# Linear attention inside a three-block kernel: blocks of 32 tokens centred on their middle, a predicated copy for the mask, three span levels above

## What is computed

```
A[t, s] = sum over d of  q[t, d] * k[s, d] * exp(c[t, d] - c[s, d])     for s <= t, else 0
out[t]  = sum over s of  A[t, s] * v[s]
```

## Time and profile before

| | us |
|---|---|
| runs, median (lowest to highest) | 2513.09 (2512.47 to 2515.55) |
| the profiled execution, its own time | 2516.41 |
| its span | 2514.6 |
| PE busy | 2092.3 (83%) |
| DVE busy | 513.2 (20%) |
| ACT busy | 367.6 (15%) |
| POOL busy | 318.8 (13%) |

### The profile page before, as it was taken

The page is one execution under the profiler, slowest core; times in us unless marked ns, Lnnn a source line. Parts: engine busy times, 40 slices in busy tenths (PEclk is TensorE's granted clock), DMA queues, the critical chain, the costliest instruction groups (busy, mean ns, idle before and its releaser), DMA issues.

```text
span 2514.6 us, 34562 instructions
## 1 busy us (share of the span) xinstructions
PE 2092.3 (83%) x14302; PEld 1163.0 (46%) x14303; DVE 513.2 (20%) x1073; ACT 367.6 (15%) x815; POOL 318.8 (13%) x144
## 2 busy tenths in 40 slices
PE   6987778677878857988879798899979899888888
PEld 5765322122222212322238675789965546454444
DVE  1044411001111101111120464100031201241111
ACT  1231111001101100111111423100001112210001
POOL 4100122222221222212210000000000000001221
PEclk9978689889999988999989969999979999989999
DMA  9654699999998899998934635455524334249994
GB/s 320 163 202 154 254 429 416 429 426 410 415 421 355 375 429 426 377 395 346 388 125 134 228 108 201 171 163 143 159 84 147 104 126 158 103 198 364 413 413 163
DMA packets 183210, 681.36 MB, mean 271 GB/s; under 512 B 15906, under 2 KB 57139, under 8 KB 150112
## 3 DMA queue, kind: packets, MB, share of 16 engines
q1 hardware_dynamic: 179200, 670.02, 68.1%
q0 software_dynamic: 3920, 10.24, 1.7%
q10 hardware_dynamic: 16, 0.02, 0.0%
HBM read 679.18 MB, written 1.06 MB: 271 GB/s over the span
## 4 chain that ended last, share of the span: by engine, by line
PE 62%; DMA 24%; DVE 7%; ACT 3%; SPq 2%; issue 1%; POOL 1%; DVEq 0%; POOLq 0%; ACTq 0%
PE ps L749 31%; DMA scr<-in_w_mlp 11%; PE ps L1092 8%; DMA MOD<-in_w_mlp 7%; PE ps L1118 5%; DMA HTY<-in_w 2%; PE ps L1396 2%; DMA spare<-in_b_mlp 2%; PE ps L784 2%; PE ps L1129 2%; PE ps L1060 1%; PE ps L1096 1%; PE ps L890 1%; PE ps L828 1%; PE ps L1433 1%
## 5 line engine op out<-in xcount | busy, mean ns | idle before, releaser
L1092 PE MATMUL ps<-ring,scr 128*32 128x512 f32 x2208 | 304.3, 701 | 139.7 <-POOL ring L696 139.0
L749 PE MATMUL ps<-ring,HTY 128*128 128x512 f32 (+5 forms) x960 | 328.0, 503 | 6.8 <-DMA ring<-in_w_out 3.7
L696 POOL COPY ring<-scr 128x4096 f32<-128x4096 f32 x62 | 223.0, 3600 | 759.1 <-DMA scr<-in_w_mlp 616.0
L749 PEld LDWEIGHTS ps<-ring,HTY 128*128 128x128 f32 x960 | 175.3, 191 | 155.9 <-issue 141.0
L1092 PEld LDWEIGHTS ps<-ring,scr 128*32 128x32 f32 x2208 | 74.5, 123 | 364.1 <-POOL ring L696 189.5
L749 PE MATMUL ps<-HTY,ring 128*128 128x256 f32 (+1 forms) x1072 | 238.1, 385 | 1.8 <-ACT HTY L1477 1.8
L749 PEld LDWEIGHTS ps<-HTY,ring 128*128 128x128 f32 (+1 forms) x1072 | 205.4, 192 | 33.3 <-ACT HTY L1477 2.7
L2199 DVE TENSOR_SCALAR spare<-ps 128x256 f32<-128x256 f32 x46 | 19.5, 425 | 686.3 <-PE ps L1096 686.3
L1477 ACT ACTIVATE scr<-ps 128x512 f32<-128x512 f32 (+6 forms) x118 | 58.4, 497 | 504.8 <-PE ps L749 401.3
L749 PE MATMUL ps<-ring,scr 128*128 128x128 f32 (+1 forms) x1040 | 121.6, 280 | 1.4 <-DVE scr L2304 1.4
L749 PEld LDWEIGHTS ps<-ring,scr 128*128 128x128 f32 x1040 | 117.5, 192 | 5.2 <-issue 3.3
(11 more groups left out here) (426 smaller groups left out, 2000.2 us busy)
## 6 DMA issues: line engine op xcount, KB each, us to landing
scr<-in_w_mlp SPq DMA_DIRECT2D x94, 2048.0 KB, 25.3
ring<-in_w_mlp SPq DMA_DIRECT2D x34, 2048.0 KB, 20.7
MOD<-in_w_mlp SPq DMA_DIRECT2D x32, 2048.0 KB, 24.2
HTY<-in_w_mlp SPq DMA_DIRECT2D x32, 2048.0 KB, 22.1
ring<-in_w_ada SPq DMA_DIRECT2D x23, 2048.0 KB, 9.1
ring<-in_w_in SPq DMA_DIRECT2D x20, 2048.0 KB, 7.9
ring<-in_w_ff SPq DMA_DIRECT2D x16, 2048.0 KB, 9.0
ring<-in_w SPq DMA_DIRECT2D x16, 2048.0 KB, 15.9
```

What stands on the lines that cost most here:

```text
L696: pool.tensor_copy(m1_slabs[j], m1_arrivals[j]).then_inc(moved[j], 1)
L749: mm = pe.matmul(o, lhs(k), rhs(k), start=begin and k == 0, stop=end and k == nk - 1)
L1092: mm = pe.matmul(ps[C1 * c:C1 * (c + 1), 0, :], XG[:, 2 * j + i, :], m1_slabs[j][:, i, BANK * c:BANK * (c + 1)], start=j + i == 0, stop=False)
```

## The change

For block one the four lower levels (16, 8, 4 and the parts) are replaced by one product over the whole tile, with decays taken relative to the middle token of each block of 32: exp(c[t] - c[mid]) goes to the query (`QB`), exp(c[mid] - c[s]) to the key (`KB`). The product is right inside each block of 32; the spans of 64 and 32 overwrite their rectangles in the same PSUM bank. A predicated copy with an integer mask of s <= t moves what is valid into `AT`, which POOL has set to zero. Level 128 stays as it was. Block two keeps all levels and the parts.

The order moves too: DVE weighs in `between(1)`, and the gain on the gate goes to `between(2)`; ACT's exponentials stand ahead of the modulations in `between(1)`; PE's and ACT's linear products stand ahead of the modulations in `between(2)`. `STAGES` follows: four products instead of seven.

```diff
-    ("ada1b", [2] * 6, 7), ("ada1c", [2] * 2, 2), ...
+    ("ada1b", [2] * 4, 4), ("ada1c", [2] * 4, 2), ...
+CENTERED = 32
+LEVELS_OF = (WIDE[:3], LEVELS)
...
 # POOL, behind vector(3)
+            pool.wait_ge(product_free, end["in1"])
+            pool.memset(AT[1], 0.0).then_inc(zeros_ready, 1)
...
 # PE
+            def centered_products():
+                pe.wait_ge(lin["spans_weighed"], 1)
+                for h in range(2):
+                    hs = slice(64 * h, 64 * h + 64)
+                    b = bank()
+                    for tile in range(NT):
+                        for pair in range(2):
+                            c, t = P * (2 * tile + pair), slice(P * tile, P * (tile + 1))
+                            mm = pe.matmul(b[:, c:c + P], KB[hs, pair, t], QB[hs, pair, t], start=True, stop=True)
+                            for i in range(1, len(LEVELS_OF[0])):
+                                m = LEVELS_OF[0][i]
+                                for row in range(0, P, 2 * m):
+                                    n = m * (P * tile + row) // (2 * m)
+                                    mm = pe.matmul(b[row:row + m, c + row + m:c + row + 2 * m], KL[hs, i, pair, n:n + m],
+                                                   QL[hs, i, pair, n:n + m], start=True, stop=True)
+                    close(mm)
+                for h in range(2):
+                    hs = slice(64 * h, 64 * h + 64)
+                    b = bank()
+                    for pair in range(2):
+                        mm = pe.matmul(b[:, P * pair:P * (pair + 1)], KL[hs, 0, pair, :], QL[hs, 0, pair, :], start=True, stop=True)
+                    close(mm)
             def rest_of_modulation(i):
+                if i == 2:
+                    centered_products()
                 for x in range(2):
                     modulation("ada1b", 0, 4 + 2 * i + x)
-                if i == 2:
-                    linear_products(0)
...
 # ACT
+            def centered_decays():
+                act.wait_ge(lin["spans"], 1)
+                act.activation(KL[:, 0:3], KL[:, 0:3], ACT.Exp)
+                act.activation(QL[:, 0:3], QL[:, 0:3], ACT.Exp)
+                act.activation(KB, QB, ACT.Exp, scale=-1.0)
+                act.activation(QB, QB, ACT.Exp).then_inc(lin["span_exp"], 1)
+            def centered_products():
+                for h in range(2):
+                    read(NB[:, h], product().rearrange("p (t c n) -> p t c n", t=NT, c=2))
+                for h in range(2):
+                    read(AT[0][:, h:4:2, P:S], two(product(), P))
             def rest_of_modulation(i):
+                if i == 1:
+                    centered_decays()
+                if i == 2:
+                    centered_products()
                 modulation(0, 4 + 2 * i)
                 modulation(0, 5 + 2 * i)
-                if i == 1:
-                    decays(0)
-                if i == 2:
-                    linear_products(0)
...
 # DVE; spans and weigh_spans now run over LEVELS_OF[n]
+            def weigh_centered():
+                weigh_spans(0, GQ, GK)
+                step(dve.tensor_tensor(KB, KB, GK, ALU.mult))
+                tell(dve.tensor_tensor(QB, QB, GQ, ALU.mult), lin["spans_weighed"], 1)
...
+            def merge_centered():
+                dve.wait_ge(product_free, end["ada1b"])
+                dve.wait_ge(zeros_ready, 6)
+                shape = [P, 2, 2, P]
+                for tile in range(NT):
+                    a = AT[tile][:, :, 0:P].rearrange("p (c h) n -> p h c n", h=2)
+                    tell(dve.copy_predicated(a, INCL.unsqueeze(1).unsqueeze(1).to_broadcast(shape), NB[:, :, tile]), lin["merged"], tile + 1)
             def between_windows(i):
                 if i == 0:
+                    middle = centered(CUM)[:, :, :, CENTERED // 2 - 1:CENTERED // 2].to_broadcast([P, 2, S // CENTERED, CENTERED])
+                    step(dve.tensor_tensor(centered(QB), centered(CUM), middle, ALU.subtract))
                     spans(0, CUM)
-                    parts(0, CUM)
+                    step(dve.tensor_tensor(INCL, tri[:, :], ident[:, :], ALU.add))
                 if i == 1:
+                    weigh_centered()
+                if i == 2:
                     gh = GG.rearrange("p a (h d) -> p a h d", h=4)
                     step(dve.tensor_tensor(gh, gh, gla_norm.unsqueeze(1).unsqueeze(1).to_broadcast([P, NT, 4, P]), ALU.mult))
-                if i == 2:
-                    weigh_parts(0, GQ, GK)
-                    weigh_spans(0, GQ, GK)
                 if i == 3:
-                    merge(0, end["ada1b"])
+                    merge_centered()
```

More of the change, by code:

```diff
@@ L55 @@
 LEVELS = WIDE + NARROW
+CENTERED = 32
+LEVELS_OF = (WIDE[:3], LEVELS)
 STAGES = [
     ("ada1a", [2] * 4, 0), ("rel", [], 1), ("h1T", [], 4), ("in1", [2, 3, 2, 2, 2], 0), ("gate1", [], 1), ("flip", [], 5),
-    ("ada1b", [2] * 6, 7), ("ada1c", [2] * 2, 2), ("mix1T", [], 4), ("out1", [3, 1], 0), ("h2T", [], 4), ("route1", [], 1), ("rank1", [], 1),
+    ("ada1b", [2] * 4, 4), ("ada1c", [2] * 4, 2), ("mix1T", [], 4), ("out1", [3, 1], 0), ("h2T", [], 4), ("route1", [], 1), ("rank1", [], 1),
     ("x1T", [], 4), ("convw", [], 1), ("in2", [4, 3, 2, 2, 2, 2], 0), ("cmp2", [1, 1], 3), ("ada3", [2] * 6, 7), ("ada3b", [2] * 2, 3),
@@ L317, in build @@
         NP = shaped(HTY[:, 0:D], (len(NARROW) * NT, 4, P // 2))
-        lin_tiles = [{"QN": carve(10496, 2, 2, P), "tmp": carve(11008, 4 * P), "squares": carve(11520, NT, BANK), "diag": carve(12544, NT, 4, PART)},
+        QB, KB, INCL = carve(10496, 2, S), shaped(HTY[:, D + 4 * P:2 * D], (2, S)), carve(11008, P).bitcast(mybir.dt.int32)
+        NB = shaped(HTY[:, 0:D], (2, NT, 2, P))
+        lin_tiles = [{"squares": carve(11520, NT, BANK)},
                      {"QN": carve(5376, 2, 2, P), "tmp": carve(5888, 4 * P), "squares": carve(5888, NT, S), "diag": carve(3008, NT, 4, PART)}]
@@ L904, in linear_products @@
             def linear_products(n):
-                pe.wait_ge(lin["parts_weighed"], n + 1)
+                pe.wait_ge(lin["parts_weighed"], 1)
                 b = bank()
@@ L1549, in decays @@
                 act.activation(lin_tiles[n]["QN"], lin_tiles[n]["QN"], ACT.Exp).then_inc(lin["span_exp"], 1)
-                act.wait_ge(lin["parts"], n + 1)
+                act.wait_ge(lin["parts"], 1)
                 act.activation(LD, LD, ACT.Exp).then_inc(lin["part_exp"], 1)
@@ L2001, in spans @@
             def spans(n, cum):
-                for i, m in enumerate(LEVELS):
+                for i, m in enumerate(LEVELS_OF[n]):
                     left, right = halves(cum, m)
@@ L2007, in spans @@
                     ins = dve.tensor_tensor(span_queries(n, i), right, last, ALU.subtract)
-                    step(ins) if m > PART else tell(ins, lin["spans"], n + 1)
+                    step(ins) if m != LEVELS_OF[n][-1] else tell(ins, lin["spans"], n + 1)
             def weigh_spans(n, q, k):
                 dve.wait_ge(lin["span_exp"], n + 1)
-                for i, m in enumerate(LEVELS):
+                for i, m in enumerate(LEVELS_OF[n]):
                     step(dve.tensor_tensor(span_keys(i), span_keys(i), halves(k, m)[0], ALU.mult))
                     ins = dve.tensor_tensor(span_queries(n, i), span_queries(n, i), halves(q, m)[1], ALU.mult)
-                    step(ins) if m > PART else tell(ins, lin["spans_weighed"], n + 1)
+                    step(ins) if n == 0 or m > PART else tell(ins, lin["spans_weighed"], n + 1)
+            def weigh_centered():
+                weigh_spans(0, GQ, GK)
+                step(dve.tensor_tensor(KB, KB, GK, ALU.mult))
+                tell(dve.tensor_tensor(QB, QB, GQ, ALU.mult), lin["spans_weighed"], 1)
             def later(x, pair):
@@ L2030, in parts @@
                                            ALU.subtract))
-                tell(dve.tensor_scalar(LD, LD, 0.0, None, ALU.min), lin["parts"], n + 1)
+                tell(dve.tensor_scalar(LD, LD, 0.0, None, ALU.min), lin["parts"], 1)
             def weigh_parts(n, q, k):
-                dve.wait_ge(lin["part_exp"], n + 1)
+                dve.wait_ge(lin["part_exp"], 1)
                 for pair in range(2):
@@ L2037, in weigh_parts @@
                     ins = dve.tensor_tensor(LD[:, pair], LD[:, pair], earlier(k, pair), ALU.mult)
-                    step(ins) if pair == 0 else tell(ins, lin["parts_weighed"], n + 1)
+                    step(ins) if pair == 0 else tell(ins, lin["parts_weighed"], 1)
             def merge(n, products):
@@ L2106, in _, with centered @@
             log_sigmoid_sums(1, GZ, GL[:, :, :], CUM, 1.0 / 16.0)
+            def centered(x):
+                return x.rearrange("p c (b j) -> p c b j", j=CENTERED)
+            def merge_centered():
[5 more added lines that the diff above has]
+                    tell(dve.copy_predicated(a, INCL.unsqueeze(1).unsqueeze(1).to_broadcast(shape), NB[:, :, tile]), lin["merged"], tile + 1)
             def between_windows(i):
```

(11 more changed lines are left out.)

## The result

The changed kernel is faster. Its five runs have a median of 2499.53 us (2493.85 to 2501.57), the kernel before beside them 2514.55; the ratio is 0.9936, 95% interval 0.992 to 0.9952, which is 16.1 us (12 to 20). Two more sets of five runs of the same kernel, each against runs of the kernel before made beside it, gave 0.9912 (0.9898 to 0.9925) and 0.9947 (0.9934 to 0.996). The mean of the three is 0.9932, some 17 us. The sets come from several chips, so versions of different sets are best compared by their ratios. The forecast was 24.1 us less (2489.0), with 17.5 us as its own lower end. The stated range ended at 2499.0; it was made against a median of 2513.09, on which the ratio gives 2497.0. That is inside the stated range, but above the forecast's own 2484.7 to 2495.6, which had a chance of 0.74. The direction and the mechanism were right, the size was too large by about 7 us.

A forecast was written before the change was run, and what follows sets the result against it. PE was taken to set the pace in this stretch, except for a stall on ACT at unit 1 and slow linear products. The terms sum to 24.1 us saved, 2489.0 us; own range 2484.7 to 2495.6, stated range 2483 to 2499.

The forecast's parts named there:

- (a): Unit 1: ACT's four exponentials run ahead of the modulations at no cost, and PE's stall goes; 5.63 us saved.
- (b): `scores(3)`, without the idle time before it, runs at the full clock; 1.79 us saved.
- (c): DVE's weighing in `between(1)` ends at 143.8, PE asks at 147.9; 4 us to spare.
- (d): The new linear products on PE take 7.2 us instead of 20.74; 13.54 saved, bounds 10.3 and 15.9.
- (e): The modulations of `between(2)` take 8.77 us instead of 8.53; a loss of 0.24.
- (f): Unit 2's transposes and values run at the full clock, 3.98 us instead of 6.69; 2.71 saved.
- (g): The modulations of `between(3)` take 8.1 us instead of 8.77, range 7.49 to 8.77; 0.65 saved.
- (h): Merge: two predicated copies of 512 columns replace 12 operations, 0.7 us each, and do not count.
- (i): POOL's memset of 512 columns runs while POOL has nothing to do; zeros are needed only after 165 us.
- Every small record drains: Rival: each of the 72 product records waits for the one before; products 32.9 us, whole time 2518; slower, chance 0.03.
- Clock: Rival: PE stays at 1.2 GHz from the products into `between(3)`; 2495 to 2497 us; 0.15 together with half-way draining.
- Hidden anyway: Rival: expert loads are memory-bound from before `mix_ready`, so the time stays at 2513 us; no change, chance 0.03.

The follow-up runs named there:

- sorted version: The changed kernel with the new matmuls of each bank sorted by size, all 128 columns, then 64, then 32; median 2491.12 us, ratio 0.9902.
- the order alone: The kernel before with all six levels and the parts, in the new order on ACT, DVE and PE; median 2509.25 us, ratio 0.9978.

## Why the forecast was right in kind and too large

**(a), (b)** held to a tenth: 134.00 to 136.28 and 145.64 to 147.92 are both 2.28 us, so 5.63 saved; `scores(3)` 1.94 against 3.73, 1.79 saved. ACT's exponentials ran under the modulation (136.81 to 139.41) and cost nothing.

**(c)** held: DVE ended its weighing at 146.08, 3.7 us before PE began at 149.78 without a wait (4 us forecast).

**(d)** is the term that was mis-sized: 7.2 us forecast, 9.07 measured, inside the bounds of 4.8 and 10.4. That a new size starts only when the last record is almost done was right, but the price of a change was put too low at both clocks: a group of 128, 64 and 32 columns takes 0.85 us at the full clock (0.70 by the forecast's 0.6 of 1.16) and 1.36 at the half clock (154.96 to 156.32; 1.16 forecast). PE's timeline of the changed kernel in narrow windows, one record each, at the half clock:

```profile
154.96 0.58 PE L1024 MATMUL ps<-scr,HTY 64*128 64x128 f32 x1
155.33 0.42 PE L1024 MATMUL ps<-scr,HTY 64*128 64x128 f32 x1
155.68 0.36 PE L1029 MATMUL ps<-spare,H 64*64 64x64 f32 x1
155.84 0.31 PE L1029 MATMUL ps<-spare,H 64*64 64x64 f32 x1
```

The last record of a size counts as forecast, 0.35 (155.33 to 155.68) and 0.24 us (155.84 to 156.08). What the sum left out is the first one: behind a change the first 128 holds the next back by 0.37 us, not by the pace of 0.21, and the first 64 by 0.16, not 0.11. Those two make the 0.20 us that are missing in each group. The forecast took its pace as a mean over eight records, in which one slow first record hardly counts. The sorted version shows the price of the changes as a whole. The clock fell midway, as the forecast allowed.

**(e)** 167.61 - 158.85 = 8.76 against 8.77. **(f)** 4.08 instead of 3.98, 2.61 saved. **(g)** 9.15 (171.69 to 180.84) instead of 8.1: the clock fell behind unit 2, so 0.38 lost, not 0.65 saved; that is 0.4 beyond the 8.77 that bounded it. **(h)** A predicated copy of 512 columns took 0.735 us, 0.7 forecast, and was hidden. **(i)** The memset took 0.52 us at 113 us, and nobody waited for it.

So the stretch gave 24.1 - 1.9 - 0.1 - 1.0 = 21.1 us. At L760 the changed kernel was 20.8 us ahead, at the end of the profiled execution 15.2: by the prediction's last sign, that the gap at L760 be there at the end, it held only in part. The remaining 4 to 5 us between the stretch and the measured 16 to 17 are of two kinds. First, the stretch of before is itself not fixed: in its second execution it was 76.4, because the values of unit 2 (from 188.28) ran at the full clock:

```profile
188.28 2.00 PE L890 MATMUL ps<-scr 128*128 128x64 f32 x16 [1.11 <-ACT scr L1539]
190.21 1.95 PE L828 MATMUL ps<-ring,cols 128*32 128x128 f32 x64
...
201.68 1.33 PE L953 MATMUL ps<-scr,H 128*128 128x128 f32 x10
```

The earlier trace rows have 3.24 us for that L828. With the mean of both executions (77.9) and of the three of the changed kernel (58.6) the stretch gives 19.3. The forecast took one execution's clock for the kernel's. Second, from L953 to the loop the changed kernel needs 73.9, 73.4 and 74.0 us in its three executions, the kernel before 73.3 and 72.0; in the changed kernel's first the product with `w_out` takes 29.6 us where the kernel before took 27.7 (from 219.03), with PE at the half clock at its start. That is about 1 us less again, and a result near 18. It is no property of the change: the sorted version needs 72.0 us there, the old levels in the new order 74.4. The rest is within the scatter of the loop and of what follows, which 15 runs don't resolve further.

So the time came out at 2497.0, in the part beyond 2495.6 that had a chance of 0.15, but by neither of the two reasons given for it: the clock was not held low through `between(2)`, and the products took 9.07 us for 72 records, 0.13 a record, not 0.2 to 0.35. It was the price of the changes and the clock behind unit 2, together with terms that the sum did not have, the scatter of the clock in the kernel before and behind the stretch. That the stated range still held it owes something to its width.

The sentence that the loop's length stays was right as far as these executions go: they don't tie it to its start. *Every small record drains* was wrong, though its direction was the one that the forecast missed. *Clock* was half right: it fell, and in the modulations it came back. *Hidden anyway* was wrong, since the time fell.

## What to carry to other kernels

Where matmuls of several sizes go into one bank, write all of one size before the next, and let matmuls in different halves of the rows, with a bank each, alternate: here both together were worth 7 us more, beside some 17 for the whole redesign, and the sorting alone 4. Thin work on PE was better placed in front of dense work than in front of work that pauses: behind it the low clock ended in the first dense piece in every execution, and in the pauses in one of four. And a saving read from one profiled execution should be checked against a second one before the last few us are believed: the same kernel's stretch differed by 3 us, and the order alone gave 12.0 us in the stretch and 5.5 in the whole time.

## What was not expected of the hardware

- Each change between matmuls of 128, 64 and 32 columns cost about 0.15 us at the full clock: 2 x 1.34 of the 4.09 us between 9.07 and 4.98. The rest is the clock's fall, which the sorted products don't meet. Part of the price is paid by the first record behind a change, 0.37 us to the next at the half clock where the pace is 0.21.
- Sixteen records of 64 rows by 128 columns in alternating row halves and two banks took 1.16 us, the same as eight in one half and one bank.
- Moving 9 us of PE work past 7.5 us of other PE work, with no wait in either order, changed the stretch by 3.9 us in one execution of each order.
- One kernel's whole time scatters by 11 us (2491.0 to 2502.2 over 15 runs of the changed kernel); the expert loop took 1001 to 1008 us.
